# Turning float32 matmuls into high and low part products in the projections of a three-block kernel

## The reference

```python
cond = silu(c)
for i in range(2):
    sh1, sc1, g1, sh2, sc2, g2 = split(cond @ ada_w[i] + ada_b[i], 6)
    h = rmsnorm(x, norm_mix[i]) * (1 + sc1) + sh1
    if i == 0:
        y = windowed_gqa(h, a_w_in, a_w_out, a_sink)     # 16 query heads, 4 key heads of 64
    else:
        y = dilated_attention(h, b_w_in, b_w_out)        # 3 groups of 8 query heads, 2 key heads
    x = x + g1 * y
    h = rmsnorm(x, norm_ffn[i]) * (1 + sc2) + sh2
    x = x + g2 * swiglu(h, ffn_w_in[i], ffn_w_out[i])

def windowed_gqa(h, w_in, w_out, sink):
    q, k, v = split(h @ w_in)                            # 1024, 256, 256 columns
    o = banded_attention(q, k, v, 128, slopes, 1, sink)  # |t - s| <= 128
    return o @ w_out                                     # 1024 x 1024

def dilated_attention(h, w_in, w_out):
    q, k, v = split(h @ w_in)                            # per group: 512, 128, 128 columns
    for each group (window 128, 512, 2048; dilation 1, 4, 16):
        outs, lses += banded_attention(strided q, k, v)
    alpha = softmax(stack(lses), axis=0)                 # share of each group, per token and head
    o = sum over groups of alpha * outs                  # 1024 x 512
    return o @ w_out                                     # 512 x 1024
```

## Time and profile before

| what | us |
|---|---|
| median of three executions | 3133.14 |
| lowest, highest | 3130.87, 3135.41 |
| the profiled execution | 3132.01 |
| its span in the profile | 3130.2 |
| PE busy (share of the span) | 2906.5 (93%) |
| DVE busy | 1391.1 (44%) |
| ACT busy | 725.3 (23%) |
| POOL busy | 271.5 (9%) |

### The profile page before, as it was taken

How to read it: one execution, slowest core, us unless ns; L and a number is a source line. 1 busy time by engine, 2 the same in 40 slices (tenths; PEclk the granted TensorE clock), 3 DMA queues, 4 the chain that set the end, 5 groups by cost and what they waited for, 6 DMA issues and landing times.

```text
span 3130.2 us, 31533 instructions
## 1 busy us (share of the span) xinstructions
PE 2906.5 (93%) x12786; PEld 2165.0 (69%) x12786; DVE 1391.1 (44%) x2359; ACT 725.3 (23%) x1167; POOL 271.5 (9%) x429
## 2 busy tenths in 40 slices
PE   2999989799999999889997779999999998999798
PEld 2444444688888888766675247888888887878767
DVE  4466651443334443555565551333323336432544
ACT  1233430211111111234444022111111114111042
POOL 2001000000000000100000000000000007941000
PEclk7999989999999999989999589999999998999899
DMA  5122131022222222210012001111111112112202
GB/s 196 41 69 74 54 128 48 23 85 90 85 67 80 78 81 82 74 28 21 23 32 81 0 27 54 41 53 54 40 54 40 54 47 81 47 41 49 74 27 74
DMA packets 139314, 187.73 MB, mean 60 GB/s; under 512 B 25088, under 2 KB 114448, under 8 KB 138928
## 3 DMA queue, kind: packets, MB, share of 16 engines
q1 hardware_dynamic: 124624, 134.33, 13.0%
q0 software_dynamic: 14592, 52.07, 5.4%
HBM read 172.62 MB, written 12.58 MB: 59 GB/s over the span
## 4 chain that ended last, share of the span: by engine, by line
PE 88%; DVE 7%; ACT 2%; issue 2%; DMA 1%; SPq 0%; DVEq 0%; ACTq 0%
PE psum L958 54%; PE psum L946 6%; PE psum L1013 6%; PE psum L1044 3%; PE psum L1007 3%; PE psum L1072 3%; PE psum L1056 2%; PE psum L1009 2%; PE psum L1008 2%; PE psum L1197 1%; DVE arena L1700 1%; PE psum L1262 1%; PE psum L985 1%; DMA hT<-in_x_dram 1%; PE psum L1323 1%
## 5 line engine op out<-in xcount | busy, mean ns | idle before, releaser
L958 PE MATMUL psum<-hT_high,w_low 128*128 128x512 f32 x2304 | 680.7, 392 | 2.1 <-DVE arena L2086 2.1
L958 PEld LDWEIGHTS psum<-hT_high,w_low 128*128 128x128 f32 x2304 | 436.2, 190 | 94.2 <-DVE arena L2086 2.3
L958 PE MATMUL psum<-hT_high,w_high 128*128 128x512 f32 x1408 | 438.5, 393 | 26.5 <-DVE h_low L1761 14.6
L958 PE MATMUL psum<-h_low,w_high 128*128 128x512 f32 x1408 | 436.5, 391 | 0.0
L1924 DVE TENSOR_TENSOR arena<-arena,psum 128x1024 f32<-128x1024 f32 x44 | 53.7, 1221 | 645.4 <-PE psum L958 645.4
L958 PEld LDWEIGHTS psum<-hT_high,w_high 128*128 128x128 f32 x1408 | 265.5, 189 | 85.7 <-DVE w_low L1916 12.7
L958 PEld LDWEIGHTS psum<-h_low,w_high 128*128 128x128 f32 x1408 | 266.6, 189 | 55.9
L1934 DVE SCALAR_TENSOR_TENSOR xT<-psum,mod,xT 128x1024 f32<-128x1024 f32 x176 | 224.2, 1282 | 163.2 <-PE psum L958 163.1
L1495 ACT ACTIVATE w_high<-wpair 128x2048 fp32r<-128x2048 f32 x62 | 118.9, 1918 | 516.1 <-DMA wpair<-in_ffn_w_out_dram 346.2
L958 PE MATMUL psum<-hid_high,w_low 128*128 128x512 f32 x768 | 236.5, 389 | 0.0
L958 PE MATMUL psum<-hid_high,w_high 128*128 128x512 f32 x704 | 217.3, 390 | 0.0
(11 more groups left out here) (270 smaller groups left out, 3383.8 us busy)
## 6 DMA issues: line engine op xcount, KB each, us to landing
wpair<-in_ffn_w_in_dram SPq DMA_DIRECT2D x44, 1024.0 KB, 5.0
arena<-in_ada_w_dram POOLq DMA_DIRECT2D x48, 512.0 KB, 4.0
wpair<-in_ffn_w_out_dram SPq DMA_DIRECT2D x22, 1024.0 KB, 4.8
wpair<-in_ada_w_dram POOLq DMA_DIRECT2D x16, 1024.0 KB, 5.8
wpair<-in_w_in_dram SPq DMA_DIRECT2D x24, 512.0 KB, 3.7
arena<-in_ada_w_dram POOLq DMA_DIRECT2D x4, 2048.0 KB, 25.8
out_dram<-xT SPq DMA_DIRECT2D x16, 512.0 KB, 5.9
xT<-out_dram SPq DMA_DIRECT2D x2, 4096.0 KB, 12.8
```

Source lines behind the costliest of these rows:

```text
L958: mm = nc.tensor.matmul(dst[:, HALF * t:HALF * t + HALF], w(k), src(k)[:, HALF * t:HALF * t + HALF], start=first and n == 0 and w is high ...
```

## The change

All matmuls of the first layer's projections, of both output projections and of the spreading of the shares become split products. The projection weights are now three tiles of 128x1024 for each unit (`kv`, `q0`, `q1`), loaded in turn into buffers 1 and 0. The output projections have tiles of the same size: eight in the first layer, four in the second. Their high and low parts are made by `tile_highs` (ACT) and `tile_lows` (DVE), whose places in the steps are given by `split_at`: steps 1, 4 and 7 of a unit for `q0` and `q1` of the next unit and `kv` of the one after it; in the last unit of a layer, steps 1 and 2 (first layer) or 1, 2 and 3 (second) for tiles of the output projection.

The first layer's residual is now also written to DRAM and read back. The order of the projection pieces is kv, kv, q0, q0, q1, q1 (before: kv, kv, q0, q1, q0, q1). The attention outputs and the shares are split as well, chunk by chunk.

```diff
-PIECES = (("kv", 0), ("kv", 1), ("q0", 0), ("q1", 0), ("q0", 1), ("q1", 1))
-BANK_USES = (("kv0", "q00", "v", "q01"), ("kv1", "q10", "q11"))
+PIECES = (("kv", 0), ("kv", 1), ("q0", 0), ("q0", 1), ("q1", 0), ("q1", 1))
+BANK_USES = (("kv0", "q00", "v", "q10"), ("kv1", "q01", "q11"))
...
-    mix(range(4))
+    mix(MIX_TILES[0])
+    for m in range(KC):
+        s.add(("wo", 0, m), (1, 0, 2)[m % 3], ("wo", 0, m))
+    ffn(0)
+    mix(MIX_TILES[1])
     for n in range(4):
-        s.add(("wo", 0, n), (2 + n) % 3, ("wo", 0, 2 * n + 1))
-    ffn(0)
-    mix(range(4, 10))
-    s.last[2] = ("q1", 9)
-    for n in range(2):
-        s.add(("wo", 1, n), (2 + n) % 3, ("wo", 1, 4 * n + 3))
+        s.add(("wo", 1, n), (2, 1, 0)[n % 3], ("wo", 1, 2 * n + 1))
...
+        def split_at(t, last):
+
+            u, n = t // 8, t % 8
+            if u + 1 < last and n in (1, 4):
+                return ("q0" if n == 1 else "q1"), u + 1
+            if u + 2 < last and n == 7:
+                return "kv", u + 2
+            if u + 1 == last and n in (1, 2, 3) and n < (3 if u < 4 else 4):
+                return "wo", int(u >= 4), n - 1
+            return None
...
+            for k in range(KC):
+                d, _, freed = ACC[("x", k)]
+                sp.wait_ge(acc_free[d], freed + 1)
+                sp.dma_start(x_kept[:, k, :], xT[:, k, :]).then_inc(x_stored, 16)
...
+            def tile_of(name, k):
+
+                pe.wait_ge(tile_split, SPLITS.index(name) + 1)
+                _, high, low = tile_parts(name)
+                return (v.rearrange("p (k n) -> p k n", k=k) for v in (high, low))
...
-                    if u >= 4:
-                        _, high, low, _ = mix_weights("kv" if what == "kv" else "q", u)
-                        ...
-                    else:
-                        ...
-                        mm = nc.tensor.matmul(dst, w[:, k, cols], hT[:, k, rows], start=k == 0, stop=k == KC - 1)
+                    high, low = tile_of((what, u), KC)
+                    rows = slice(HALF * half, HALF * half + HALF)
+                    nc.tensor.matmul(dst, high[:, k, :], hT_high[:, k, rows], start=k == 0, stop=False)
+                    nc.tensor.matmul(dst, high[:, k, :], h_low_mix[:, k, rows], start=False, stop=False)
+                    mm = nc.tensor.matmul(dst, low[:, k, :], hT_high[:, k, rows], start=False, stop=k == KC - 1)
...
+            def project_o(layer, m, chunks, tile, at):
+
+                dst, ready = take(("wo", layer, m))
+                high, low = tile_of(tile, chunks)
+                wait = (lambda k: pe.wait_ge(o_split, KC * layer + k + 1)) if m == 0 else None
+                split_products(dst, range(chunks), lambda k: high[:, k, at:at + P], lambda k: low[:, k, at:at + P],
+                               lambda k: o_high[layer][k], lambda k: o_low[layer][k], wait).then_inc(ready, 1)
...
-                    pe.wait_ge(share_ready, 1)
-                    pe.wait_ge(const_ready, 3)
+                    pe.wait_ge(share_split, g + 1)
+                    pe.wait_ge(pick_ready, 1)
                     for t in range(2):
-                        mm = nc.tensor.matmul(dst[:, HALF * t:HALF * t + HALF], pick[:, m, :], lseT[:, g, HALF * t:HALF * t + HALF], start=True, stop=True)
+                        cols = slice(HALF * t, HALF * t + HALF)
+                        nc.tensor.matmul(dst[:, cols], pick_high[:, m, :], share_high[:, g, cols], start=True, stop=False)
+                        mm = nc.tensor.matmul(dst[:, cols], pick_high[:, m, :], share_low[:, g, cols], start=False, stop=True)
...
@@ ACT, attention
-                    if u >= 4 and n == 0 and u + 1 < last:
-                        projection_high("q", u + 1)
-                    if u >= 4 and n == 4 and u + 2 < last:
-                        projection_high("kv", u + 2)
                     if t < 8 * last:
                         exponentials(t)
                     if t > 8 * first:
                         turned_copy(t - 1)
+                    name = split_at(t, last)
+                    if name:
+                        tile_highs(name)
...
@@ DVE, attention
-                    if u >= 4 and n == 0 and u + 1 < last:
-                        projection_low("q", u + 1)
-                    if u >= 4 and n == 4 and u + 2 < last:
-                        projection_low("kv", u + 2)
+                    name = split_at(t, last)
+                    if name:
+                        tile_lows(name)
                     if t < 32 and n % 2 == 0:
                         m = 4 * u + n // 2
                         piece(ada_mid, ada_acc[:, 128 * n:128 * n + 256], ada_landed[4], 16 * (m + 1), 7 * (4 + m), 4 + m)
...
@@ DVE, after the group shares are summed
             for g in range(3):
-                ins = nc.vector.tensor_tensor(lseT[:, g], lseT[:, g], esum, ALU.mult)
-            ins.then_inc(share_ready, 1)
+                nc.vector.tensor_tensor(lseT[:, g], lseT[:, g], esum, ALU.mult).then_inc(share_ready, 1)
+            for g in range(3):
+                dve.wait_ge(share_high_ready, g + 1)
+                nc.vector.tensor_tensor(share_low[:, g, :], lseT[:, g, :], as_f32(share_high[:, g, :]), ALU.subtract).then_inc(share_split, 1)
...
+                if m:
+                    o_lows(1, m - 1)
+            o_lows(1, 3)
```

More of the change, by code:

```diff
@@ L149, in piece_of @@
     what, half = PIECES[i // KC]
-    return what, half, {"kv": half, "q0": 0, "q1": 1}[what], what + str(half)
+    return what, half, what + str(half)
 def units():
@@ L580, in load_mix @@
                 sp.dma_start(kv[:, :, DH:P], rows[:, :, cv:cv + DH]).then_inc(landed, 16)
-                load(("q", u), rows[:, :, cq:cq + 256], KC)
             def load_ffn(l):
@@ L1032, in scores @@
                 if n == 0:
-                    pe.wait_ge(proj_free[pair], bank_use(pair, f"q{pair}1", u) + 1)
+                    for half in range(2):
+                        pe.wait_ge(proj_free[half], bank_use(half, f"q{pair}{half}", u) + 1)
                     pe.wait_ge(k_ready, 4 * (u + 1))
@@ L1178, in _ @@
             modulation_sums(dst, ada_sum).then_inc(ready, 1)
-            norm(1)
             ffn(0)
@@ L1428, in projection_high, with tile_highs @@
-            def projection_high(what, u):
-                s, _, landed = WTS[(what, u)]
-                whole, high, _, _ = mix_weights(what, u)
+                l, at = n // 2, 24 * (n % 2)
+                for k in range(KC):
+                    act.wait_ge(scaled, KC * n + k + 1)
+                    whole = h_whole if n % 2 else h_whole_mix
+                    nc.scalar.activation(hT_high[:, k, :], whole[:, k, :], ACT.Identity, bias=mod[:, l, at + k:at + k + 1]).then_inc(shifted, 1)
+            def tile_highs(name):
+                s, _, landed = WTS[name]
+                whole, high, _ = tile_parts(name)
@@ L1466, in attention @@
             def attention(first, last):
+                tile_highs(("q1", first))
                 for half in range(2):
-                    for m in range(2):
-                        queries(first, m, half)
-                if first == 4:
-                    projection_high("kv", 5)
+                    queries(first, 0, half)
+                tile_highs(("kv", first + 1))
+                for half in range(2):
+                    queries(first, 1, half)
                 for t in range(8 * first, 8 * last + 1):
@@ L1550, in _ @@
             attention(0, 4)
-            norm(1, lambda k: copied(("wo", 0, k)))
+            act.wait_ge(o_read, 32)
+            for k in range(KC):
+                nc.scalar.activation(o_high[0][k], LAY[0]["oT"][:, k, :], ACT.Copy).then_inc(o_high_ready, 1)
+            tile_highs(("wo", 0, 2))
+            norm(1, lambda k: copied(("wo", 0, k)), lambda k: tile_highs(("wo", 0, k + 3)) if k + 3 < KC else None)
             ffn(0)
```

240 lines of the change are left out of this document (122 added, 118 removed).

## The result

The changed kernel takes 3154.3 us (median of 4 runs, 3153.6 to 3159.9), the kernel before on the same chip 3133.7 us (3130.9 to 3135.4). The ratio is 1.0071, 95% interval 1.0053 to 1.0088: slower by 21 us, where 27 were predicted. The profiled execution took 3153.6 us with a span of 3151.6.

A forecast was written before the change was run, and what follows sets the result against it. PE was taken to bound the kernel, with a chain through ACT and DVE in each layer's last unit. The terms sum to +26.9 us on the profiled 3132.01 us, forecast 3160 us, range 3143 to 3178 us.

The forecast's parts named there:

- What would show it: List of signs expected in the changed kernel's profile, such as unit 5 at 69 to 72 us instead of 62.0.
- 1 start: Start of the first layer: DVE makes two low parts ahead of the norm, which writes in two parts; +5.7 us.
- 6 first output projection with its start: First layer's output projection: 128 cheaper matmuls, less 2.5 us until the first chunk is split; -20.5 us.
- Step 2: Projections of units 1 to 3: 3 x 48 replaced matmuls, each giving 0.180 us; -25.9 us.
- Step 3: PE waiting for split tiles in units that project: +27.7 us in the first layer, +25.7 us net in the second.
- Step 5: Low clock of PE after 14 waits of 2 us or more, 1.4 us each; +19.6 us.
- Step 4: Last unit of each layer: a longer chain through ACT and DVE; +11.0 us in unit 3, +9.1 us in unit 9.
- Step 7: Norms between output projection and feed-forward: new buffer order gives +4.0 us in the first, -4.0 in the second; total 0.
- Step 8: Shares and second layer's output projection: DVE becomes the bound, 77.5 us instead of 103.0; -25.5 us.
- the paragraph on prices: Float32 matmul 0.861 us, fp32r 0.227, three of these 0.681; each replaced matmul gives 0.180 us, with 272 matmuls counted.
- The fast rival: In attention, ACT makes high parts early enough, so PE's waits for splits vanish: 3063 us; chance 0.07.

The follow-up runs named there:

- H: The changed kernel with ACT's high parts in attention moved ahead of the exponentials of their step; 3064.3 us, ratio 0.979 to the kernel before.

## Why the prediction was right

Direction, time and cause came out as said: 3154.3 us is inside my own range of 3143 to 3178. The signs listed under "What would show it" are in the profile but for one size: DVE's splits waiting for ACT in attention (27 places, 4.0 us each for about 3), PE's 2.9 us for `kv` where the projection of units 6 to 9 starts (in the timeline that is the start of units 5 to 8), 5.82 us in the middle of units 0 to 2, unit 5 at 71.5 us, units 1 and 2 at 85.1 and 83.3, the first output projection at 88.9, the two projections and the shares 51 us shorter. Shares and second projection came at 72.0 us, not 78. By steps, predicted and measured on the profiled executions:

| step | predicted | measured |
|---|---|---|
| 1 start | +5.7 | +4.6 |
| 2, 3, 5 units 0 to 2 | -25.9 + 27.7 + 7.0 = +8.8 | +11.1 |
| 3, 5 units 4 to 8 | +25.7 + 12.6 = +38.3 | +34.7 |
| 4 unit 3 | +11.0 | +8.3 |
| 4 unit 9 | +9.1 | +11.7 |
| 6 first output projection with its start | -20.5 | -18.3 |
| 7 norms | 0 | +4.2, -4.0, -1.6 |
| 8 shares and second projection | -25.5 | -29.9 |
| sum | +26.9 | +20.8 |

The spans of the two profiled executions differ by 21.4 us. The steps miss by 1 to 4.4 us each, five low and three high, so the sum is closer than its parts by some luck; no step that was priced has the wrong sign.

- Step 2 is clean in H, where no wait hides it: units 0 to 2 take 216.8 us against 241.3, -24.5 for 25.9 predicted.
- Step 3, waits: units 4 to 8 have 25.2 us of idle PE in the changed kernel and none in H, for 29.5 predicted: `kv` 2.9 (3.0), `q1` 1.8 (2.4), `q0` 0.5 to 1.2 (1.1). In units 0 to 2 it is 25.1 us more than in H, for 27.7: `q1` 5.8 (6.5), `q0` 2.2 in unit 0 and 0.8 in units 1 and 2 (1.4). For `kv` the size was right (2.3 for 2.0), the queue was not: PE waits at the scores for DVE's modulation (L1735) behind the split, and has the tile by then.
- Step 5: the busy time of PE in units 4 to 8 is 13.6 us above H, for 12.6 predicted; in units 0 to 2 it is 10.5 us above H, for 7.0. The total is 24.1 for 19.6, and the price for each wait does not hold: unit 6 loses 0.7 us after the same waits that cost unit 7 4.9.
- Step 4 was right in sum (20.0 measured for 20.1) and wrong in its parts; as unit 3 differs by up to 3.6 us by itself, that the sum fits is luck in part. In unit 9 three waits of 4.12, 2.58 and 2.58 us at a clock of 0.60 cost more than the links I added up, and without them 2 us of the unit's growth remain (36.0 in H against 34.1).
- Step 7 swapped as said.
- Step 8 is the term furthest off, by 4.4 us. From the first spreading matmul to the norm it takes 72.0 us (1869.2 - 1797.2), not 77.5: DVE needs 30.9 us to the third chunk of the projection. I had 34.5 to the last one: the low part of the last chunk (1.2 us) is made while PE multiplies the third, and 1.3 us of the shares' low parts lie before the first matmul. The last two chunks and seven products then take 41.1 us; I had 43.0 with the last chunk alone.
- The waits for semaphores that have long passed, up to 5 us in the prediction, cost nothing: unit 5 takes 62.02 us in H and in the kernel before. The 272 matmuls of the paragraph on prices leave out the 64 of the second output projection; no term of the sum uses that number.

The fast rival ("the splits are hidden", 3063 us) was wrong for this kernel and nearly right as arithmetic: H takes 3064.3, though the term for shares and second projection misses by 4.3 us in H too. Its mechanism failed where the change puts the high parts, at the end of ACT's step.

## What to carry to other kernels

Cheaper matmuls bring new work on the engines that feed them, and what that costs is set by its place in their queues: an instruction that depends on nothing belongs ahead of the ones that wait for PE. Find the place by asking what stands between PE's last result and the new instruction, and count every link behind it. When the releaser named in a wait is an engine with idle time just before its instruction, go back one more link, and price a wait with the slower products behind it.

## What the runs showed of the hardware

- The granted clock can be low while PE is busy without a break. Matmuls of 8 rows (8 partitions of both operands) began at 1.00 (0.23 us apart) behind 108 matmuls of 128 rows and a wait of 1.04 us, and ran at 0.50 (0.43 us apart) some 4 us later; in float32, 41.3 us of them without a break stayed at 0.50, while at the start of unit 7, where most matmuls have 128 rows, the products were 0.23 us apart again 6.4 us after the wait. I had put the low clock of the earlier trace rows down to the idleness before it; that is not enough.
- The same wait does not always cost clock. Unit 6 kept it behind 2.88 and 1.94 us of waiting (0.7 us lost), unit 7 lost it behind 2.88 (4.9 us with its other waits); a wait of 1.83 us in unit 4 (1428.40) left it at 1.00, one of 1.83 us in unit 5 (1498.33) was followed by products 0.43 us apart. What decides between them is open.
- With 11 matmuls in such a wait the products behind it ran at 1.00 at four of four places; without them that was so for all nine products in unit 6 alone. In the idleness before the shares matmuls ran at the high clock from the first on (80 in 18.4 us).
